# Second block: the mean square ahead of the gate-up norm, from three means made during the output projection

## The reference

```
h = _rmsnorm(x, pre_mix_norm[l])
h = _hybrid_mixer_2(h, ...)                 # ends in  mixed @ w_out
x = x + _rmsnorm(h, post_mix_norm[l])
h = _rmsnorm(x, pre_ffn_norm[l])
h = _conv_glu_ffn(h, ffn_up[l], ...)        # starts with  h @ ffn_up
x = x + _rmsnorm(h, post_ffn_norm[l])
```

## Time and profile before

| | us |
|---|---|
| median of 3 runs | 1983.45 (1979.24 to 1987.24) |
| the profiled execution | 1986.72 |
| its span, first to last instruction | 1984.9 |
| PE busy | 1886.6 (95%) |
| DVE busy | 1213.2 (61%) |
| ACT busy | 993.7 (50%) |
| POOL busy | 722.7 (36%) |

### The profile page before, as it was taken

How to read it: one execution, slowest core, us unless ns; L and a number is a source line. 1 busy time by engine, 2 the same in 40 slices (tenths; PEclk the granted TensorE clock), 3 DMA queues, 4 the chain that set the end, 5 groups by cost and what they waited for, 6 DMA issues and landing times.

```text
span 1984.9 us, 40944 instructions
## 1 busy us (share of the span) xinstructions
PE 1886.6 (95%) x15728; PEld 1848.8 (93%) x15728; DVE 1213.2 (61%) x1480; ACT 993.7 (50%) x1301; POOL 722.7 (36%) x607
## 2 busy tenths in 40 slices
PE   6999999999999999999999998997999889979997
PEld 6999999999999999999999988987999789969997
DVE  5545586666556646676665566556774755657754
ACT  4434565454344444555543456455654464556542
POOL 4661211257417621302376002503661105215631
PEclk9999999999999999999999989998999889999999
DMA  6546544456455555444564532222554423215543
GB/s 227 190 150 214 176 148 147 169 183 203 163 197 204 190 177 201 143 151 150 191 203 166 187 138 93 86 86 87 199 182 161 141 101 107 86 55 179 191 152 124
DMA packets 48938, 312.33 MB, mean 157 GB/s; under 512 B 5680, under 2 KB 6832, under 8 KB 19888
## 3 DMA queue, kind: packets, MB, share of 16 engines
q1 hardware_dynamic: 48096, 307.84, 45.2%
q10 hardware_dynamic: 720, 2.84, 0.4%
HBM read 309.61 MB, written 1.05 MB: 157 GB/s over the span
## 4 chain that ended last, share of the span: by engine, by line
PE 70%; DVE 9%; ACT 8%; DMA 7%; issue 3%; POOL 2%; ACTq 0%; DVEq 0%; SPq 0%; POOLq 0%
PE ps L545 18%; PE ps L546 17%; PE ps L547 17%; DMA raw<-in_down_dram 5%; ACT w_hi L1201 5%; DVE w_lo L1682 4%; PE ps L902 3%; PE ps L550 3%; PE ps L551 3%; PE ps L552 3%; PE ps L713 1%; PE ps L753 1%; DMA raw<-in_in_dram 1%; DVE conv L2009 1%; DVE rstd L1688 1%
## 5 line engine op out<-in xcount | busy, mean ns | idle before, releaser
L1682 DVE TENSOR_TENSOR w_lo<-raw,w_hi 128x2048 fp32r<-128x2048 f32 (+1 forms) x320 | 692.4, 2164 | 360.6 <-ACT w_hi L1201 359.9
L545 PE MATMUL ps<-xn,w_hi 128*128 128x256 f32 x2688 | 763.9, 284 | 39.4 <-DVE xn L1695 26.4
L546 PE MATMUL ps<-xn,w_hi 128*128 128x256 f32 x2688 | 755.1, 281 | 0.0
L547 PE MATMUL ps<-xn,w_lo 128*128 128x256 f32 x2688 | 754.8, 281 | 0.0
L1201 ACT ACTIVATE w_hi<-raw 128x2048 fp32r<-128x2048 f32 (+1 forms) x320 | 558.9, 1748 | 151.7 <-DMA raw<-in_down_dram 89.7
L545 PEld LDWEIGHTS ps<-xn,w_hi 128*128 128x128 f32 x2688 | 517.0, 192 | 47.5 <-DVE xn L1695 22.1
L546 PEld LDWEIGHTS ps<-xn,w_hi 128*128 128x128 f32 x2688 | 515.6, 192 | 0.7 <-issue 0.5
L547 PEld LDWEIGHTS ps<-xn,w_lo 128*128 128x128 f32 x2688 | 515.2, 192 | 0.0
L545 PE MATMUL ps<-h,w_hi 128*128 128x256 f32 x1056 | 294.4, 279 | 2.5 <-DVE w_lo L1682 2.4
L547 PE MATMUL ps<-h,w_lo 128*128 128x256 f32 x1056 | 293.7, 278 | 0.0
L546 PE MATMUL ps<-h,w_hi 128*128 128x256 f32 x1056 | 293.7, 278 | 0.0
(11 more groups left out here) (328 smaller groups left out, 2684.7 us busy)
## 6 DMA issues: line engine op xcount, KB each, us to landing
raw<-in_gu_dram SPq DMA_DIRECT2D x132, 1024.0 KB, 4.9
raw<-in_in_dram SPq DMA_DIRECT2D x68, 1024.0 KB, 4.9
raw<-in_down_dram SPq DMA_DIRECT2D x96, 704.0 KB, 4.1
raw<-in_out_dram SPq DMA_DIRECT2D x16, 1024.0 KB, 4.9
raw<-in_pb_dram SPq DMA_DIRECT2D x4, 1024.0 KB, 4.7
raw<-in_pa_dram SPq DMA_DIRECT2D x4, 1024.0 KB, 4.8
tables_all<-in_tables_dram ACTq DMA_DIRECT2D x1, 1648.0 KB, 6.8
rows<-in_rows_dram SPq DMA_DIRECT2D x2, 768.0 KB, 5.4
```

What stands on the lines that cost most here:

```text
L545: pe.matmul(out, w, xh, start=first, stop=False)
L546: pe.matmul(out, w, xl, start=False, stop=False)
L547: return pe.matmul(out, wl, xh, start=False, stop=last)
L1682: dve.tensor_tensor(w_lo[:, r, 0:elems], raw[:, k % RAW_RING, 0:elems], w_hi[:, r, 0:elems], ALU.subtract).then_inc(lo.sem, 1)
```

## The change

With h the output of the projection, g the gain of the norm behind it, r the reciprocal root of that norm, the new x is x + r g h. The mean of its squares is mean(x x) + 2 r mean(x g h) + r r mean(g h g h). The changed kernel computes it by this formula:

- ACT makes two squares of each output tile, of `hm[c]` (`sq_out`) and of `g * hm[c]` (`sq_post`); POOL sums six of the eight chunks of each (four additions each, one of them of 128 x 512). DVE makes the cross product `x_post[c] = hm[c] * g * x[c]` and sums six chunks of it. PE makes three means, each with three matmuls: the sum, chunk 6 and chunk 7.
- The mean of the old x's squares is kept in `ssum` from the layer's first norm (one or two small DVE products there).
- DVE combines the four values in five dependent operations on 128 x 256. ACT takes the root, DVE the reciprocal.
- The squares of the new x (ACT) and their eight matmuls are gone.
- The addition to x and the second norm are one loop on DVE (`x_after_mix`): `add_post(c)` makes v and, for even c, the new x. `normed(c)` makes the normalised chunk.
- The load of ACT's root table (by a one-element activation) stands ahead of the tiles.
- DVE's split of gate-up slot 1 stands behind the whole of `x_after_mix`.

```diff
+    sq_out = at_byte("sq_out", [KC, T], area + 24 * KB)
+    sq_post = at_byte("sq_post", [KC, T], area + 32 * KB)
+    x_post = at_byte("x_post", [KC, T], area)
...
             out_part(3, 0, KC)
-            mean_square(at, 0)
-            mean_square_direct(at, 1)
+
+            def mean_of(part, chunk, run, out):
+                pe.wait_ge(run.sem, run.upto(at, 4))
+                pe.matmul(out, ones_d[:], part[:, 0], start=True, stop=False)
+                for c in (KC - 2, KC - 1):
+                    pe.wait_ge(chunk.sem, chunk.upto(at, c + 1))
+                    last = pe.matmul(out, ones_d[:], part[:, c], start=False, stop=c == KC - 1)
+                return last
+
+            mean_of(sq_out, out_sq, out_sq_run, ps[:, AUX, 0:T]).then_inc(mean_sq.sem, 1)
+            mean_of(x_post, cross, cross_run, ps[:, AUX + 1, T:2 * T])
+            mean_of(sq_post, post_sq, post_sq_run, ps[:, AUX + 1, 0:T]).then_inc(mean_sq.sem, 1)
             first_wide(at, st2["gu"], 0)
...
-            for j in range(4):
-                if j == 1:
+            act.activation(warm[:, 0:1], eps[:, 0:1], ACT.Sqrt)
+            for c in range(KC):
+                if c == 2:
                     split(at, so.slot0 + 2 + LEAD, 0, SLOT)
-                square(at, 0, 2 * j, hm[:, 2 * j])
-                square(at, 0, 2 * j + 1, hm[:, 2 * j + 1])
-            root(at, 1)
+                act.wait_ge(x_new.sem, x_new.upto(at, c + 1))
+                act.activation(sq_out[:, c], hm[:, c], ACT.Square).then_inc(out_sq.sem, 1)
+                act.activation(sq_post[:, c], hm[:, c], ACT.Square, scale=gains2[:, 4 * layer + 1, c:c + 1])\
+                   .then_inc(post_sq.sem, 1)
+            root(at, 1, T, False)
             split(at, so.slot0 + 3 + LEAD, 0, SLOT)
-            for c in range(KC):
-                x_ready(act, at, 0, c)
-                act.activation(sq8[:, c], x[:, c], ACT.Square).then_inc(squared.sem, 1)
-            root(at, 2)
+            act.wait_ge(next_mean.sem, next_mean.upto(at, 5))
+            act.activation(rms[:, 0:T], sqb[:, 0], ACT.Sqrt).then_inc(rooted.sem, 1)
...
                     inverse(at, 0)
+                    if layer:
+                        dve.tensor_tensor(ssum[:], rms[:, 0:T], rms[:, 0:T], ALU.mult).then_inc(x_mean.sem, 2)
+                if k == 5 and layer == 0:
+                    for n in range(2):
...
+                        dve.tensor_tensor(ssum[:], ssum[:], sqb[:, 0], ALU.mult).then_inc(x_mean.sem, 1)
...
+            def cross_of(c):
+                dve.wait_ge(x_new.sem, x_new.upto(at, c + 1))
+                dve.scalar_tensor_tensor(x_post[:, c], hm[:, c], gains2[:, 4 * layer + 1, c:c + 1], x[:, c],
+                                         ALU.mult, ALU.mult).then_inc(cross.sem, 1)
...
+                tile_done(dve, at, so, c // 2, c % 2)
+                dve.tensor_copy(hm[:, c], out_tile(c)).then_inc(x_new.sem, 1)
+                if c == 1:
+                    cross_of(0)
+                if 3 <= c < KC - 1:
+                    cross_of(c - 1)
+                if c == KC - 2:
+                    cross_add(2, 6, slice(2, 4), slice(4, 6))
+                    cross_add(3, 6, 2, 3)
+                    cross_of(c)
+            cross_of(KC - 1)
+            cross_add(4, 6, 0, 2)
...
+            def x_after_mix():
+
+                inverse(at, 1)
...
+                nm = sqb[:, 0]
+                dve.wait_ge(mean_sq.sem, mean_sq.upto(at, 3))
+                dve.tensor_tensor(nm, ps[:, AUX + 1, 0:T], rstd[:, 0:T], ALU.mult).then_inc(next_mean.sem, 1)
...
+                dve.scalar_tensor_tensor(nm, ps[:, AUX + 1, T:2 * T], 2.0, nm, ALU.mult, ALU.add)\
...
+                dve.tensor_tensor(nm, nm, rstd[:, 0:T], ALU.mult).then_inc(next_mean.sem, 1)
...
+                dve.tensor_tensor(nm, nm, ssum[:], ALU.add).then_inc(next_mean.sem, 1)
...
+                dve.tensor_scalar(nm, nm, EPS, None, ALU.max).then_inc(next_mean.sem, 1)
+                add_post(0)
+                add_post(1)
+                dve.wait_ge(rooted.sem, rooted.upto(at, 3))
+                dve.reciprocal(sqb[:, 1], rms[:, 0:T]).then_inc(rstd_ok.sem, 1)
+                dve.wait_ge(rstd_ok.sem, rstd_ok.upto(at, 3))
+                normed(0)
+                add_post(2)
+                for c in range(1, KC):
+                    normed(c)
+                    if c < KC - 2:
+                        add_post(c + 2)
+                    if c % 2:
+                        low_even(at, 0, c - 1)
...
-            post(1)
+            x_after_mix()
             split(at, so.slot0 + 3 + LEAD, 0, SLOT)
-            inverse(at, 2)
-            for c in range(KC):
-                dve.scalar_tensor_tensor(v[:, c], x[:, c], gains2[:, 4 * layer + 2, c:c + 1], rstd[:, 0:T],
-                                         ALU.mult, ALU.mult).then_inc(v_ok.sem, 1)
...
-            add_squares(at, 0)
+            part_add(sq_out, out_sq, out_sq_run, 1, 2, 0, 1)
+            part_add(sq_post, post_sq, post_sq_run, 1, 2, 0, 1)
+            for part, chunk, run in ((sq_out, out_sq, out_sq_run), (sq_post, post_sq, post_sq_run)):
+                part_add(part, chunk, run, 2, 6, slice(2, 4), slice(4, 6))
+                part_add(part, chunk, run, 3, 6, 2, 3)
+                part_add(part, chunk, run, 4, 6, 0, 2)
             add_odd(at, 0)
             for c in range(1, KC, 2):
                 low(at, 0, c)
```

More of the change, by code:

```diff
@@ L334, in program @@
     x_odd = sig("x_odd", 0, KC)
+    out_sq = sig("out_sq", 0, KC)
+    post_sq = sig("post_sq", 0, KC)
+    cross = sig("cross", 0, KC)
+    out_sq_run = sig("out_sq_run", 0, 4)
+    post_sq_run = sig("post_sq_run", 0, 4)
+    cross_run = sig("cross_run", 0, 4)
+    x_mean = sig("x_mean", 0, 2)
+    next_mean = sig("next_mean", 0, 5)
     projected = sig("projected", 20, 8)
-    squared = sig("squared", 3 * KC, 4 * KC, pre=KC, mid=KC)
-    summed = sig("summed", 21, 7, pre=7)
+    squared = sig("squared", 3 * KC, 2 * KC, pre=KC, mid=KC)
+    summed = sig("summed", 21, 0, pre=7)
     first_sum = sig("first_sum", 0, 0)
@@ L554, in mean_square @@
         def mean_square(at, k, by_token=False):
-            pe.wait_ge(summed.sem, summed.upto(at, 7 * (k + 1) if at[0] == 2 else 7 * k))
+            pe.wait_ge(summed.sem, summed.upto(at, 7 * k))
             if by_token:
@@ L1145, in _ @@
             down(at, st2["down"], 0, st2["gu"])
-            mean_square_direct(at, 2, AUX, DOWN_ADDED, down_sum)
+            mean_square_direct(at, 0, AUX, DOWN_ADDED, down_sum)
     def slot_done(eng, at, st, j, g=0):
@@ L2116, in _ @@
                     inverse(at, 0)
+                    if layer:
+                        dve.tensor_tensor(ssum[:], rms[:, 0:T], rms[:, 0:T], ALU.mult).then_inc(x_mean.sem, 2)
+                if k == 5 and layer == 0:
+                    for n in range(2):
+                        if n:
+                            dve.wait_ge(x_mean.sem, x_mean.upto(at, n))
+                        dve.tensor_tensor(ssum[:], ssum[:], sqb[:, 0], ALU.mult).then_inc(x_mean.sem, 1)
                 if k == 1:
@@ new lines, in cross_add @@
+            def cross_add(n, have, to, more):
+                dve.wait_ge(cross.sem, cross.upto(at, have))
+                if n > 1:
+                    dve.wait_ge(cross_run.sem, cross_run.upto(at, n - 1))
+                dve.tensor_tensor(x_post[:, to], x_post[:, to], x_post[:, more], ALU.add).then_inc(cross_run.sem, 1)
+            for c in range(KC):
+                if c == 2:
+                    cross_of(1)
+                    cross_add(1, 2, 0, 1)
+                    split(at, so.slot0 + 2 + LEAD, 0, SLOT)
+                tile_done(dve, at, so, c // 2, c % 2)
[8 more added lines that the diff above has]
+                    cross_of(c)
@@ L2290, in add_of_down @@
             for c in range(1, DOWN_ADDED):
-                pool.wait_ge(squared.sem, squared.upto(at, 2 * KC + c + 1))
+                pool.wait_ge(squared.sem, squared.upto(at, c + 1))
                 if c > 1:
@@ L2433, in _, with part_add @@
                 .then_inc(o_lo.sem, 1)
-            add_squares(at, 0)
+            def part_add(part, chunk, run, n, have, to, more):
+                pool.wait_ge(chunk.sem, chunk.upto(at, have))
+                if n > 1:
+                    pool.wait_ge(run.sem, run.upto(at, n - 1))
+                pool.tensor_tensor(part[:, to], part[:, to], part[:, more], ALU.add).then_inc(run.sem, 1)
+            part_add(sq_out, out_sq, out_sq_run, 1, 2, 0, 1)
[4 more added lines that the diff above has]
+                part_add(part, chunk, run, 4, 6, 0, 2)
             add_odd(at, 0)
@@ L2443, in x_square @@
                 def x_square(c):
-                    pool.wait_ge(squared.sem, squared.upto(at, 3 * KC + c + 1))
+                    pool.wait_ge(squared.sem, squared.upto(at, KC + c + 1))
                     if c > 1:
```

24 lines of the change are left out of this document (16 added, 8 removed).

## The result

The changed kernel takes 2002.58 us (median of 3 runs, 2000.47 to 2014.19) against 1983.45: ratio 1.0097, 95% interval 1.0056 to 1.0137. The same kernel was run again in two later comparisons with 12 runs each beside 35 and 29 of before; these gave 1.0040 [1.0016, 1.0065] and 1.0034 [1.0008, 1.0061], so 7 to 8 us. It is slower, by less than the first comparison says.

A forecast was written before the change was run, and what follows sets the result against it. PE, 95% busy, was taken as the bound, so only its idle or low-clock time counted. Layer 0 +2.8 and layer 1 +3.8 gave +6.6 us on the 1983.45 median: 1990.0 us, range 1981 to 1997.

The forecast's parts named there:

- Tile 7's copy: DVE copy of the last output tile: 1.3 us late from taking turns with POOL's sums, bounds 0 to 2.4.
- Start of the combination: From tile 7's copy to DVE's first combining operation: 1357.0 in layer 0, set by POOL's sums and three matmuls.
- This one ends last: Before the combination: POOL's `sq_post` sums, ending about 1355.5, plus three matmuls end at 1357.0, after the other arm's 1356.6.
- 1.3 more: Extra us that the three matmuls behind POOL's sums would take if PE ran at 1.2 GHz.
- Five operations: DVE's dependent combining operations: 2.6 us including 0.13 gaps, ending at 1359.6, bounds 2.1 to 3.1.
- Second reciprocal: On DVE behind `add_post(0)` and `add_post(1)`, which end at 1360.9: reciprocal and gap 1.90, done at 1362.8.
- Chunk 0: First gate-up chunk: six DVE operations, 2.5 us, so PE starts at about 1365.4, 3.2 us earlier than before.
- POOL's queue: Low part 1 stands behind all four odd additions: PE gets chunk 1 at 1372.6 after idling some 6 us.
- The rest of slot 0: 42 gate-up matmuls, first 4.6 us at 1.2 GHz: slot 0 ends at 1379.5 against 1376.7, +2.8 in layer 0.
- the clock rival: PE at 1.2 GHz from the third mean through all slot 0: +13.4 us, 1996.9; chance 0.23 including any miss above +9.9.
- Costed at nothing: Work assumed hidden, such as DVE's split of slot 1 behind the loop: ended by 1376.9, wanted at 1379.5, covered by 2.6.
- The floor named there: End of DVE's split of gate-up slot 1, at 1377: limits what the change can win if PE is faster.

The follow-up runs named there:

- y3: Changed kernel with one operand of the cross products of tiles 2 to 7 read from PSUM instead of SBUF: ratio to the kernel before 1.0037.
- x1: Changed kernel with POOL's low parts interleaved with its additions: slot 1 starts 2.7 and 1.4 us earlier than in the changed kernel run again.
- x3: Changed kernel with 16 unused matmuls behind the third mean and 12 between chunks 0 and 1: timed gain 0.08% on the changed kernel.
- z1: y4 with chunk 7's low part made by DVE ahead of its split of slot 1: median 1988.79 against the changed kernel's 1993.16, ratio to before 0.998.
- z2: z1 without the 16 unused matmuls: median 1986.42 against the changed kernel's 1993.16, ratio to before 0.999.
- y2: Changed kernel with POOL's low parts interleaved and 16 unused matmuls ahead of slot 0: median 1985.88 against before's 1987.13, ratio interval 0.9995 to 1.0047.
- y4: Changed kernel with cross-product operand from PSUM, POOL's low parts interleaved and 16 unused matmuls ahead of slot 0: level with the kernel before.

## Why the prediction was wrong

It gave 1990.0 and 1981 to 1997; 2002.58 came. In the size of the effect, 0.33%, it agrees with the two longer comparisons (0.34% and 0.40%). But its sum of +6.6 us is some 3 short of what the stretches show (+9.2 to +10.2), and the range left no room for the scatter of a median of three runs. The agreement with the two comparisons is partly luck: they are good to some 5 us either way, and in the sum errors of both signs cancel, most of all in layer 1 (slot 1 at 41.1, predicted 40.6). Step by step, offsets from tile 0's copy:

1. *Tile 7's copy.* Predicted 13.6, measured 14.7. **This step failed in size**: 2.5 us late, at its upper bound of 2.4, not 1.3. The product of tile 6 did lose its turn to POOL's second sum (1.48), and both sums of DVE took turns (1.99 together). y3 confirms the turns: with an operand in PSUM the products beside sums of 512 take 0.48.
2. *Start of the combination.* "This one ends last" named POOL's arm with three matmuls behind it: 18.1. Measured 21.2 and 19.5. **This step failed in its mechanism.** It named two arms and left out a third, the product and the sum of `x_post` on DVE behind tile 7's copy. POOL was done at 1355.3 as forecast (1355.5), but the mean of `x_post` stands ahead of the third in PE's queue and waited for DVE's last sum until 1355.65. So six matmuls remained, not three: 2.9 us to the first operation in layer 1, 4.6 with the low clock of layer 0, where 1.6 was predicted. The "1.3 more" at 1.2 GHz was named, and left out of the sum.
3. *Five operations.* Predicted 2.6, measured 2.05 (1360.24 to 1362.29): they follow each other at 0.46, a gap of 0.04 where 0.13 was assumed, and the last one, short, makes way after 0.21. The Trainium skill, VectorE: DVE Perf Modes, section on the DRAIN, has a semaphore behind each operation cost nothing extra. Here a dependent operation follows at 0.46, an independent one after 0.40 behind a product and 0.33 behind an addition, so by these rows a dependence costs about 0.1, and that rule came nearer than my gap.
4. *Second reciprocal.* From the start of the combination to n0: 5.1 measured, 5.8 predicted. The order on DVE was as told. This 0.7 hid part of the miss of step 2.
5. *Chunk 0.* 26.5 predicted, 28.9 and 27.2 measured; from n0 on it is 2.6, as predicted (2.5).
6. *POOL's queue.* Right. v7 was done 7.8 us after n0's start (predicted 8.0), PE ran six matmuls and waited 5.43 (some 6). x1 shows the cause.
7. *The rest of slot 0.* Predicted 6.9, measured 7.5 and 6.9 (7.6 in y3). The clock rose 5.5 us after chunk 1 in layer 0, not 4.6. But the clock rival's other half came true: 1.2 GHz already in the third mean of layer 0. x3 prices the low clock at 2.4 and 2.5 us a layer against x0_again, at 3.9 and 1.5 against the first profile.

*Costed at nothing.* The split of slot 1 ended at 1378.8, before PE's 1382.4: covered, as said. The floor named there, the end of this split, is what z1 and z2 ran into. Of the signs that were named, two came out otherwise: a sum of 128 x 512 on DVE read 1.12 instead of 1.2 or more, and PE waits for `w_lo` 4.1 us in all from 1506 us on, where before it was 2.4.

The likeliest cause (POOL's order pays back what DVE won) was right, but not the whole. Mending that order alone (x1) or holding the clock alone (x3) leaves 5.6 and 4.8 us of excess, and both together (y2) still 4.5. Two more costs had to go before the stretch was as short as before: products that take turns with POOL (y4), and chunk 7's low part beside a split (z1).

How far the excess of the first three runs over 8 us was slow spells stays open: only one of them has a trace, and in that one 5.7 of the 15.9 us lie outside the stretches.

## What to carry to other kernels

Where work moves off the matrix engine's path and onto a vector engine, count the new operations there together with those of the engine that it takes turns with (here DVE with POOL, where an operation has two operands in SBUF), and walk the waiting engine's own queue: what stands ahead of the awaited matmul counts, not only what it waits for. A chain that is shortened at its start gives nothing if the last piece, here the low parts behind additions in a fixed order, keeps its place. A difference of half a per cent needed a dozen runs on each side here; three were off by 10 us.

## What the runs showed of the hardware

- TensorE has two paces at a granted clock of 1.00: 356 and 342 matmuls of 256 columns in 40 us, in spells of some 40 to 200 us at places that change from run to run. Their cause is not shown.
- A product of DVE on 128 x 256 with two operands in SBUF takes 0.48 alone, 0.95 beside an addition of POOL on 128 x 256, and 1.16 and 1.48 beside its sums of 128 x 512 (after). With one of them in PSUM it takes 0.48 beside a sum of 128 x 512, twice, and 0.47 beside an addition of 128 x 256 (y3).
- The other way round, a subtraction of POOL that takes 0.91 takes 2.59 when a split of 2048 elements on DVE (2.28) has begun 0.27 before it (y2), and ends 0.6 after it. The Trainium skill, GPSIMD Engine Reference, section Specifications, says that GpSimd's SBUF interfaces are shared with VectorE, with contention for instructions with two SBUF inputs, and gives no price; these runs agree with it.
